# Mixer A's norms tile by tile inside mixer B, index dots block by block, and the sigmoid product on DVE

## The reference, cut to what matters

```python
h = einsum('btd,de->bte', rms_norm(x), w_in)      # qa ka va ua qi ki wi qb kb vb ub ga gb
qa, ka = rope(rms_norm(qa)), rope(rms_norm(ka))   # per head of 64
score = einsum(relu(qi . ki), wi)                 # top-k keys of each row: 128 of up to 512 (72 of 288)
A = softmax over the chosen keys (qa . ka) @ va
a = sigmoid(z) * running_product(sigmoid(-z))     # z = qb . kb, from the last key backwards
B = a @ vb
y = x + (sigmoid(ga) * ((A*silu(ua)) @ w_a) + sigmoid(gb) * ((B*silu(ub)) @ w_b)) @ w_o
```

## Time and profile before

| | before |
|---|---|
| median of 3 runs | 573.23 us (571.34 to 573.59) |
| the profiled execution | 572.14 us, of it a span of 570.4 us |
| PE busy | 539.1 us, 95% of the span |
| DVE, ACT, POOL busy | 323.1, 222.4, 76.4 us |
| mean granted clock of PE | 0.973 of full speed |

### The profile page before, as it was taken

How to read it: one execution, slowest core, us unless ns; L and a number is a source line. 1 busy time by engine, 2 the same in 40 slices (tenths; PEclk the granted TensorE clock), 3 DMA queues, 4 the chain that set the end, 5 groups by cost and what they waited for, 6 DMA issues and landing times.

```text
span 570.4 us, 10220 instructions
## 1 busy us (share of the span) xinstructions
PE 539.1 (95%) x4344; PEld 511.8 (90%) x4344; DVE 323.1 (57%) x650; ACT 222.4 (39%) x354; POOL 76.4 (13%) x87
## 2 busy tenths in 40 slices
PE   4999699999999999989969799999999999999998
PEld 3889699999999999979969788898899999999997
DVE  5805647788987886734763456663245433456331
ACT  7614645215445456423403666643413323123110
POOL 4313000001342222160450000000000000000000
PEclk9999989999999999987979899999899999999999
DMA  8611202541102220240422005021033222227311
GB/s 329 239 74 38 85 1 74 183 160 64 51 37 76 75 75 1 75 148 1 153 74 75 2 1 180 22 75 38 1 111 111 75 60 90 75 94 280 140 49 50
DMA packets 15214, 50.45 MB, mean 88 GB/s; under 512 B 2400, under 2 KB 5856, under 8 KB 11584
## 3 DMA queue, kind: packets, MB, share of 16 engines
q1 hardware_dynamic: 15168, 49.79, 24.7%
HBM read 42.82 MB, written 6.82 MB: 87 GB/s over the span
## 4 chain that ended last, share of the span: by engine, by line
PE 86%; DVE 5%; POOL 3%; ACT 3%; issue 2%; DMA 1%; SPq 0%; ACTq 0%; DVEq 0%
PE PS L506 34%; PE PS L723 13%; PE PS L784 9%; PE PS L766 8%; PE PS L460 4%; PE PS L638 4%; PE PS L617 3%; PE PS L492 3%; POOL nrs L1584 2%; PE PS L561 2%; PE PS L593 2%; PE PS L701 2%; ACT whi L830 1%; PE PS L454 1%; DVE wlo L1111 1%
## 5 line engine op out<-in xcount | busy, mean ns | idle before, releaser
L506 PE MATMUL PS<-xhi,whi 128*128 128x272 f32 x320 | 94.9, 297 | 5.7 <-DVE q_flat L1216 5.3
L1111 DVE TENSOR_TENSOR wlo<-raw,whi 128x2048 fp32r<-128x2048 f32 (+1 forms) x36 | 74.4, 2068 | 36.0 <-ACT whi L830 35.9
L506 PE MATMUL PS<-xlo,whi 128*128 128x272 f32 x320 | 93.2, 291 | 0.0
L506 PE MATMUL PS<-xhi,wlo 128*128 128x272 f32 x320 | 92.7, 290 | 0.0
L830 ACT ACTIVATE whi<-raw 128x2048 fp32r<-128x2048 f32 (+1 forms) x36 | 61.7, 1718 | 76.8 <-PE PS L723 33.7
L506 PE MATMUL PS<-whi,xhi 128*128 128x256 f32 x256 | 77.3, 302 | 3.9 <-DVE oT L1304 3.3
L506 PE MATMUL PS<-wlo,xhi 128*128 128x256 f32 x256 | 75.3, 294 | 0.0
L506 PE MATMUL PS<-whi,xlo 128*128 128x256 f32 x256 | 74.7, 292 | 0.0
L506 PEld LDWEIGHTS PS<-xhi,whi 128*128 128x128 f32 x320 | 60.9, 190 | 9.3 <-DVE q_flat L1216 5.6
L506 PEld LDWEIGHTS PS<-xhi,wlo 128*128 128x128 f32 x320 | 61.0, 191 | 0.0
L506 PEld LDWEIGHTS PS<-xlo,whi 128*128 128x128 f32 x320 | 60.9, 190 | 0.0
(11 more groups left out here) (204 smaller groups left out, 1135.2 us busy)
## 6 DMA issues: line engine op xcount, KB each, us to landing
raw<-in_w_units SPq DMA_DIRECT2D x28, 1024.0 KB, 4.9
stage<-in_x_kw_qi SPq DMA_DIRECT2D x8, 564.0 KB, 7.2
raw<-in_w_mixes SPq DMA_DIRECT2D x8, 512.0 KB, 3.5
res<-in_x_kw_qi SPq DMA_DIRECT2D x1, 2176.0 KB, 8.0
out<-res SPq DMA_DIRECT2D x16, 136.0 KB, 1.7
out<-vals SPq DMA_DIRECT2D x2, 1024.0 KB, 5.4
out<-kT SPq DMA_DIRECT2D x1, 1088.0 KB, 6.5
out<-tm SPq DMA_DIRECT2D x1, 1024.0 KB, 4.3
```

Of the source, the lines that this page charges most:

```text
L506: mm = pe.matmul(out, lhsT, rhs, start=(k == 0), stop=(k == 23))
L1111: dve.tensor_tensor(wlo[:, uu % 2, 0:n], raw[:, uu % 2, 0:n], whi[:, uu % 2, 0:n].bitcast(F32), ALU.subtract).then_inc(w_lo, 1)
```

## The change

The order of the units changes: `ub0` moves ahead of `kb0`, and `ka0`, `ka1` ahead of `ub1`. Four groups of `vb1` instead of two come before the dots. The dots run block by block (eight heads of block 3, then 2, 1, "s"), with a group after every four, and from block 2 on a top-k round of block 3 after every second dot. The additions of a block now follow each other in one sum. The rest of top-k is spread so that the blocks with most rounds to do come first. The squares of keys and queries go into slots 11 to 15 and 25 to 29 on ACT, their sums one slot later on DVE, the roots one more later on POOL by tile; scaling, gain and rotation follow in slots 19 to 24 (keys) and 33 to 38 (queries). The product `weights` moves from POOL to DVE, behind the step's first group. The queries' transposes come before the last two groups of `va0`, and the store of the new keys before the loads of `ua1` and `va0`.

```diff
-UNITS = [(n, KIND[n[:2]]) for n in ("vb0", "vb1", "kb1", "kb0", "qb0", "qb1", "ub0", "ub1", "ka0", "ka1", "qa0", "qa1",
+UNITS = [(n, KIND[n[:2]]) for n in ("vb0", "vb1", "kb1", "ub0", "kb0", "qb0", "qb1", "ka0", "ka1", "ub1", "qa0", "qa1",
-DOT_FILL = groups_of("vb1")[2:] + groups_of("kb1") + groups_of("kb0")[:1]
-B_FILL = groups_of("qb1", "ub0", "ub1", "ka0", "ka1", "qa0", "qa1")
+DOT_FILL = groups_of("vb1")[4:] + groups_of("kb1") + groups_of("ub0")[:3]
+DOTS_PER_FILL = 4
+PRE_B = groups_of("ub0")[3:] + groups_of("kb0", "qb0")
+B_FILL = groups_of("qb1", "ka0", "ka1", "ub1", "qa0", "qa1", "ua0")[:B_SLOTS]
+POST_B = groups_of("ua0")[2:] + groups_of("ua1", "va0")
-K_SUM_STEPS = (11, 12, 13)
+K_SLOT, Q_SLOT = 11, 25
-DOTS = [(h, b) for h in range(H) for b in SCORED]
+DOTS = [(h, b) for b in SCORED for h in range(H)]
...
+            for g in POST_B[:2]:
+                group(g)
             for n in K_ITEMS:
                 item(n)
-            unit("ua1")
-            unit("va0")
+            for g in POST_B[2:-2]:
+                group(g)
             pe.wait_ge(q_rows, 1)
             for n in Q_ITEMS:
                 item(n)
+            for g in POST_B[-2:]:
+                group(g)
...
+            def square_tile(t, c, k, name):
                 n = TILES[t][1]
+                group_out_wait(act, FIRST_GROUP[U[name]] + t)
+                if k >= 1:
+                    act.wait_ge(summed_up, k)
+                act.activation(square[0:n, :], tm[0:n, t, c:c + W], ACT.Square).then_inc(squared, 1)
...
                 if t < N_STEPS:
                     sigmoids(t)
                 filled(mine[0])
+                squares(2 * t)
                 if 1 <= t <= N_STEPS:
                     turned(t - 1, aT, at_done, pv_done, at_out)
                 filled(mine[1])
+                squares(2 * t + 1)
...
+            for n, (h, b) in enumerate(DOTS):
+                dve.wait_ge(relu_done, n + 1)
...
+                    dve.wait_ge(acc_done, n)
+                    dve.scalar_tensor_tensor(scores(b), r, w, scores(b), ALU.mult, ALU.add).then_inc(acc_done, 1)
...
+                if n % DOTS_PER_FILL == DOTS_PER_FILL - 1:
+                    fill(DOT_FILL[n // DOTS_PER_FILL])
+                if b != 3 and n % 2:
+                    topk(3)
...
+            def weights(t):
+                dve.wait_ge(scan_done, t + 1)
+                dve.wait_ge(sig_done, t + 1)
+                n = step_width(t)
+                v = sig[:, t % 2, :, 0:n - 1]
+                dve.tensor_tensor(v, v, rest[:, t % 2, :, 1:n], ALU.mult).then_inc(a_done, 1)
...
+            def mean_squares(t, k):
+                dve.wait_ge(squared, k + 1)
+                link(dve.tensor_reduce(nss[0:n, t, :], square[0:n, :].rearrange("p (h d) -> p h d", h=H), AX.X, ALU.add))
+                dve.tensor_scalar(nss[0:n, t, :], nss[0:n, t, :], 1.0 / HD, EPS, ALU.mult, ALU.add).then_inc(summed_up, 1)
...
                 for k in range(2):
-                    filled(mine[k])
-                    topk_half()
+                    fill(mine[k])
+                    if k == 0 and t < N_STEPS:
+                        weights(t)
+                    if rounds_done != ROUNDS:
+                        topk_half()
+                        if rounds_done == ROUNDS:
+                            topk_end()
+                    norms(2 * t + k)
             weighed(PAIRS, pv_done, pv_out, PAIRS, suB)
...
+            def roots(k):
+                pool.wait_ge(summed_up, k + 1)
+                pool.tensor_tensor(nrs[0:n, t, :], nss[0:n, t, :], halves[0:n, 0:H], ALU.pow).then_inc(rooted, 1)
```

More of the change, by code:

```diff
@@ L407, in _ @@
             sp.dma_start(rows_s(new_b_v_s), vals[0:DEC, 6, :]).then_inc(st_vb, 16)
-            load_unit("ub0")
+            load_unit("ka0")
             group_out_wait(sp, LAST_GROUP[U["kb0"]])
             sp.dma_start(new_b_k_fm, kT[:, :, 0:NT]).then_inc(st_kb, 16)
-            for name in ("ub1", "ka0", "ka1", "qa0", "qa1", "ua0", "ua1", "va0"):
+            for name in ("ka1", "ub1", "qa0", "qa1", "ua0"):
                 load_unit(name)
+            sp.wait_ge(k_rows, 1)
+            sp.dma_start(rows_p(new_a_k_p), tm[:, 0:4, W:2 * W]).then_inc(st_ka, 16)
+            sp.dma_start(rows_s(new_a_k_s), tm[0:DEC, 4, W:2 * W]).then_inc(st_ka, 16)
+            load_unit("ua1")
+            load_unit("va0")
             sp.wait_ge(pv_done, N_STEPS)
@@ L550, in _ @@
                 item(n)
-            for g in groups_of("vb1")[:2]:
+            for g in groups_of("vb1")[:4]:
                 group(g)
             pe.wait_ge(item_lo, len(I_ITEMS) + 1)
[L554 to L565, removed]
+            for n, (h, b) in enumerate(DOTS):
+                if n >= 6:
+                    pe.wait_ge(relu_done, n - 5)
+                m, q, k0 = (DEC, iqS[:, h, :], SEQ) if b == "s" else (P, iqT[:, h, P * b:P * b + P], 0)
+                for c in range(2):
+                    mm = pe.matmul(ps[0:m, n % 6, 0:n_keys(b)], q, ikT[:, c, k0:k0 + n_keys(b)],
+                                   start=(c == 0), stop=(c == 1))
+                mm.then_inc(dot_done, 1)
+                if n % DOTS_PER_FILL == DOTS_PER_FILL - 1:
+                    group(DOT_FILL[n // DOTS_PER_FILL])
+            for g in PRE_B:
                 group(g)
@@ L920, in _, with filled @@
             act.activation(ikT[:, 0, SEQ:SEQ + PAST], past_i, ACT.Copy).then_inc(item_hi, 1)
[L921 to L935, removed]
-                unit_next(g)
+            def filled(g):
+                if ON_ACT[g]:
+                    evacuate(g)
+                elif UNITS[GROUPS[g][0]][0][0] == "u":
+                    sigmoid_u(g)
+                unit_next(g)
+            for g in groups_of("vb1")[:4]:
+                filled(g)
+            for n, (h, b) in enumerate(DOTS):
+                act.wait_ge(dot_done, n + 1)
+                if n >= 4:
+                    act.wait_ge(acc_done, n - 3)
+                m = DEC if b == "s" else P
+                act.activation(relus[0:m, n % 4, 0:n_keys(b)], ps[0:m, n % 6, 0:n_keys(b)], ACT.Relu,
+                               scale=HD ** -0.5).then_inc(relu_done, 1)
+                if n % DOTS_PER_FILL == DOTS_PER_FILL - 1:
+                    filled(DOT_FILL[n // DOTS_PER_FILL])
+            for g in PRE_B:
+                filled(g)
             def sigmoids(t):
@@ L1020, in _ @@
                 item(n)
-            for g in groups_of("ua1", "va0"):
+            for g in POST_B[2:-2]:
                 filled(g)
@@ L1271, in topk_half @@
                         last_step[b] = steps[0]
+                for b in live:
+                    rounds_done[b] += 1
+            def topk_half():
+                todo = sorted(SCORED, key=lambda b: rounds_done[b] - ROUNDS[b])
+                topk(*todo[:2])
             def topk_end():
+                assert rounds_done == ROUNDS
                 dve.wait_ge(topk_step, steps[0])
@@ L1387, in masked @@
+                    if rounds_done != ROUNDS:
[3 more added lines that the diff above has]
+                    norms(2 * t + k)
+            weighed(PAIRS, pv_done, pv_out, PAIRS, suB)
+            slot = B_SLOTS
+            for g in POST_B:
+                fill(g)
+                norms(slot)
+                slot += 1
+            unit_next(filling[0])
             def masked(t):
@@ L1551, in _ @@
             add_sample("vb0")
-            add_sample("vb1")
             def silu(g):
```

238 lines of the change are left out of this document (94 added, 144 removed).

## The result

The changed kernel takes 575.5 us (median, 575.0 to 578.8), the kernel before 573.2 in the same comparison (571.3 to 574.5). The ratio is 1.0065, with a 95% interval of 1.0048 to 1.0082: slower, where 569.2 us and faster were forecast.

The account below looks back on a forecast made before the run. PE was taken as busy almost throughout, losing time to waits and half clock. Recovering 28.2 us, giving back 23.2 and adding 2 for clock took the profiled 572.14 to 569.1, forecast as 569.2 us; forecast 566 to 572, wider range 561.5 to 576.

Parts of the forecast that it names:

- Two us were set aside: Over the whole kernel: 2 us added for half clock behind the new waits, bounds 0 to 9.
- Rival 2: Half clock after every new or kept wait, seven places, up to 3 us each: likely 572 to 579 us; chance 0.18.
- The recovered 28.2: Sum of old waits and half clock to be recovered: 7.2 ahead of the dots, 19.2 between mixers, 1.8 at first logits.
- The 7.2 ahead of the dots: Ahead of the index dots: 4.4 us of wait, 1.4 of half-clock dots and 1.4 for the group behind recovered.
- The 1.8 at the first logits: Mixer A's first logits: half clock recovered, 1.4 us and 0.4 on the logits beside it.
- the 19.2: Between mixer B and mixer A: 12.7 us of PE idle and 6.5 us of half clock recovered.
- The dots: Index dots: PE waits on DVE's evacuations, slowed by top-k rounds; 8.2 us lost, `kb0` starting near 118.
- Mixer B: Mixer B: DVE falls half a microsecond a step behind, late sums delay squares and `turned`; waits 3.9 and 3.3, 7.2 us lost.
- Behind mixer B: After mixer B: 1.6 us half clock kept, waits 2.4 (last weighing), 1.5 (queries' rows), 1.0 (first logits); 6.5 us lost.
- Rival 1: DVE is not late: mixer B's 7.2 us loss and some of the dots' 8.2 fall away, 558 to 565 us; chance 0.22.
- Rival 4: `ua1` arrives late behind the store; splits and last weighing wait 2 to 5 us: 571 to 574 us; chance 0.06.
- Rival 3: POOL's roots keep DVE's two-input operations waiting, 1.5 us each: 573 to 575 us; chance 0.04.

Follow-up runs that it names:

- mixer A's entry mended: Changed kernel with DVE's split of `gate0` issued behind mixer A's first masked logits instead of ahead of them: 571.62 us, ratio 0.9973 to the kernel before.

## Why the prediction was wrong

- **The step that failed: the path at mixer A's entry.** I wrote "1.0 us instead of 3.2" for the first logits, and stopped there. I had seen that the queries' turns move ahead of `va0`'s last two groups, but counted only the wait ahead of the logits, not what stands on DVE between the logits and the next copy. The move puts `gate0`'s split there: 4.0 us of wait and 1.3 of half clock. Moving only the split took 4.1 us off, and moving the transposes back 2.7. This is shown.
- **The half clock was undersized.** Two us were set aside, and the 1.6 kept behind the last weighing. Measured were 8.2: 1.8 behind the dots, 1.7 in mixer B, 2.9 behind the weighing, 1.3 in mixer A, and the rest in the waits themselves. "They are 1.3 to 3.9 us long" was read as a reason for little. Rival 2 had the sign, but not the count: low clock stands in four places, not seven. Nor does it decide alone: with mixer A's entry mended the kernel takes 0.9973 of the time before.
- **The recovered 28.2.** The 7.2 ahead of the dots came, as far as the waits and the clock show (4.4 is 1.3, and the clock is 1.00 from 66.0 to 119.3). The 1.8 at the first logits came too: the logits and the group behind them run at full clock,

```profile
319.30:323.50 4.20, 4.11 (x32) 3.61 (x32) 2.19 (x1) 1.95 (x2) 0.72 (x1) 1.00 0.00 0
```

  and the 4.38 us are the next group, behind the new wait. Of the 19.2 the old waits went (3.3, 5.3, 3.2), but 9.7 us stand in the same stretch now, for 4.9 forecast.
- **The dots: right.** 8.7 us of waits for 8.2, four on DVE's evacuations and one of 2.2 on ACT's relu, `kb0` starting at 119.3 for "near 118". Without the rounds no wait is left. The last of the five waits is 2.13 us in both profiles of the changed kernel and in that with the squares three groups later. In four others that leave this part alone it is 0.70 to 0.85, and in the one with the squares behind the turned copy there is none. The clock goes with it. Of the changed kernel, and then of the one with the queries' turns behind the groups (length, PE busy, clock):

```profile
113.90:117.20 3.30, 3.27 (x24) 1.00 0.94 341
119.30:123.30 4.00, 3.98 (x19) 0.57 0.01 4
```

```profile
114.60:118.00 3.40, 3.38 (x16) 0.57 0.92 354
119.80:124.00 4.20, 3.98 (x31) 1.00 0.01 4
```

  The clock falls behind the last wait or behind the one ahead of it; there the slower group fills what would have been the last wait, and that much of the price is swallowed. So the waits are 8.7 us in some executions and 6.6 to 7.4 in others, with nothing changed in the program here. This may be part of why the profiled executions are above the median: the two longest of the seven runs show a mean clock of 0.982, the other five 0.985 to 0.988; those were not profiled.
- **Mixer B: the right two waits, for part of the reason.** 4.7 us and 1.7 of clock for 7.2. The squares ahead of `turned` made them, as forecast, near the step forecast. But DVE was not half a microsecond a step behind. For steps 2 to 4 the prediction set DVE's 25 us against 23.6 of PE. PE takes 24.8 for them, and DVE keeps up:

```profile
161.80:186.60 24.80, 24.80 (x227) 22.94 (x226) 24.44 (x54) 14.06 (x18) 0.95 (x1) 1.00 0.13 44
```

  In step 6 DVE waits for the sigmoids:

```profile
197.31 2.34 DVE L1308 TENSOR_TENSOR_SCAN wk<-wk 128x512 f32<-128x512 f32 x2 [0.80 <-ACT wk L952]
199.69 1.23 DVE L1317 TENSOR_TENSOR wk<-wk 128x1022 f32<-128x1022 f32 x1
...
202.54 0.68 DVE L1336 TENSOR_REDUCE nss<-square 128x8 f32<-128x512 f32 x1
203.25 0.17 DVE L1337 TENSOR_SCALAR nss<-nss 128x8 f32<-128x8 f32 x1
```

  Scan, product, half a pair of rounds and sum, one behind the other, are 6 us from the sigmoid: the order in the queue makes the square late at 203.5 even with a punctual DVE. That the squares' place ahead of `turned` is the cause is shown, since with the two swapped the waits are gone. The products cost DVE 13.9 us (8.2, 4.9 and 0.8 by form) for 12.6, and the prediction's own formula gives 12.9.
- **Behind mixer B: right in the waits.** 2.9, 1.8 and 1.0 us for 2.4, 1.5 and 1.0.
- **The other rivals.** Rival 1 did not come. Rival 4 did not: nothing waits for `ua1`. Rival 3 did not as written: I find no DVE operation that a root held up. POOL's gate products held some, below.

## What to carry to other kernels

When a program's order is changed, walk every engine's queue from each moved step to the next thing that PE needs, not only to the first wait: the step that costs may be one that nobody moved, caught between two others. An operation that waits on another engine should stand behind the copy that TensorE wants, not ahead of it; here two swapped lines were worth 5 us. And an edit whose gain can't be told from nothing by itself can be worth 4 us once the other waits are gone, so a failed experiment is tried again at the end.

## What the hardware showed that I had not expected

**POOL and DVE do hold each other up.** The mid part of mixer B, DVE and then POOL (start us, us):

```profile
211.06 2.28 DVE L1108 TENSOR_TENSOR wlo<-raw,whi 128x2048 fp32r<-128x2048 f32 x1
213.25 1.52 DVE L1317 TENSOR_TENSOR wk<-wk 128x766 f32<-128x766 f32 x1
```

```profile
211.68 2.28 POOL L1586 TENSOR_TENSOR oT<-oT,silu_tmp 128x272 f32<-128x272 f32 x1 [3.59 <-ACT silu_tmp L898]
213.92 2.35 POOL L1601 TENSOR_TENSOR nrs<-nss,halves 128x8 f32<-128x8 f32 x1
217.60 0.76 POOL L1586 TENSOR_TENSOR oT<-oT,silu_tmp 128x272 f32<-128x272 f32 x1 [1.33 <-ACT silu_tmp L898]
```

POOL's gate product takes 0.76 us alone and 2.28 when it starts inside DVE's split, ending 0.6 us behind it; the root that follows takes 2.35 for 1.64, and DVE's product, which starts inside the gate product, 1.52 for 0.96. The split is as fast as ever. Another gate product, at 272.53 inside the split of 271.90, took 2.28 too. The Trainium skill, SBUF — State Buffer, "Who interferes with whom", has such an exclusion of two-input operations; for POOL behind a split this trace agrees with it, while the earlier trace rows showed a split unhindered inside a root. The other way round, DVE's short scaling of a sum (0.17 us alone) takes 0.68 when it starts inside a gate product on POOL (276.37 to 277.13), and ends with it:

```profile
276.47 0.68 DVE L1337 TENSOR_SCALAR nss<-nss 128x8 f32<-128x8 f32 x1
```

This one stands ahead of the last weighing, for which PE waits 2.9 us, so by this row some 0.5 of that wait is POOL's. Otherwise the price here is small: eight gate products of the `q_flat` form took 1.3 us on average for 0.9 before.

**A wait's length does not tell alone what the clock does.** After the waits of 2.9 to 4.0 us the groups ran at half clock; among the dots one of 2.7 us was followed by it in one execution and not in another (above). After 1.31 us ahead of the third group of `vb1` and 1.35 in mixer B they did not; after 1.11 ahead of the mixing, where PE had just done the short matmuls of a last weighing, they did (7.68 us for 6.03):

```profile
413.44 7.68 PE PS L770 x48
...
433.18 6.03 PE PS L770 x48
```
